# A four-layer encoder trunk: cross attention by products of high and low parts, one buffer for decay rows, six shared slots for weights

## What is computed

```python
def memory_cross_attention(q, mem_n, w_kv, gq, gk):
    k, v = jnp.split(mem_n @ w_kv, 2, axis=-1)
    q = rmsnorm(q.reshape(b, l, X_HEADS, X_HEAD_DIM), gq)
    k = rmsnorm(k.reshape(b, m, X_HEADS, X_HEAD_DIM), gk)
    v = v.reshape(b, m, X_HEADS, X_HEAD_DIM)
    s = jnp.einsum('blhd,bmhd->bhlm', q, k).astype(jnp.float32) * (X_HEAD_DIM ** -0.5)
    p = jax.nn.softmax(s, axis=-1).astype(v.dtype)
    return jnp.einsum('bhlm,bmhd->blhd', p, v).reshape(b, l, X_WIDTH)
```

## Time and profile before

| | us |
|---|---|
| median of three runs | 1771.86 |
| the profiled execution | 1771.1 |
| its span, first to last instruction | 1769.3 |
| TensorE busy | 1763.4 |
| VectorE busy | 1162.1 |
| ScalarE busy | 1004.8 |
| GpSimd busy | 220.8 |
| low parts of weights on VectorE, 569 of 1.226 us | 691.9 |
| casts of weights on ScalarE, 569 of 1.060 us | 597.0 |

### The profile page before, as it was taken

One profiled execution on the slowest core, in us unless ns is written; L12 is line 12 of the kernel. 1 busy time (PEld: TensorE's weight loads), 2 busy tenths in 40 slices (PEclk: granted clock), 3 DMA queues, 4 the chain that ended last, 5 costly groups with the idle time before them and its releaser, 6 DMA issues.

```text
span 1769.3 us, 25818 instructions
## 1 busy us (share of the span) xinstructions
PE 1763.4 (100%) x9492; PEld 1519.9 (86%) x9492; DVE 1162.1 (66%) x1596; ACT 1004.8 (57%) x1598; POOL 220.8 (12%) x548
## 2 busy tenths in 40 slices
PE   9999999999999999999999999999999999999999
PEld 8998988888888888888888888888899998888887
DVE  5788875655665665666666546666678887556665
ACT  6667775544455675544465545444566777545443
POOL 3412231000012230000012300000131223100000
PEclk9999999999999999999999999999999999999999
DMA  8565543566555443565655445666556554356663
GB/s 285 165 209 183 179 144 124 176 199 191 191 175 176 161 143 119 181 200 190 189 192 196 161 131 174 199 190 193 182 169 205 184 165 156 129 190 191 190 191 131
DMA packets 90041, 314.03 MB, mean 177 GB/s; under 512 B 10176, under 2 KB 11584, under 8 KB 89920
## 3 DMA queue, kind: packets, MB, share of 16 engines
q1 hardware_dynamic: 89328, 311.27, 54.4%
q10 hardware_dynamic: 592, 1.12, 0.2%
HBM read 311.23 MB, written 1.11 MB: 177 GB/s over the span
## 4 chain that ended last, share of the span: by engine, by line
PE 96%; DVE 2%; ACT 1%; issue 0%; DMA 0%; SPq 0%; DVEq 0%; ACTq 0%
PE ps L1229 19%; PE ps L1231 19%; PE ps L1230 19%; PE ps L1251 13%; PE ps L1258 7%; PE ps L1240 3%; PE ps L1241 3%; PE ps L1242 3%; PE ps L1396 2%; PE ps L1376 2%; PE ps L1327 1%; PE ps L1276 1%; PE ps L1286 1%; DVE w_lo_t L1669 1%; DVE xsT L1752 1%; DVE bcT L1752 1%
## 5 line engine op out<-in xcount | busy, mean ns | idle before, releaser
L1669 DVE TENSOR_TENSOR w_lo_t<-raw,w_hi_t 128x1024 fp32r<-128x1024 f32 x569 | 691.9, 1226 | 387.9 <-ACT w_hi_t L1425 387.4
L1425 ACT ACTIVATE w_hi_t<-raw 128x1024 fp32r<-128x1024 f32 x569 | 597.0, 1060 | 394.6 <-PE ps L1231 146.9
L1229 PE MATMUL ps<-w_hi_t,act_hi 128*128 128x512 f32 x832 | 329.2, 396 | 0.0
L1230 PE MATMUL ps<-w_lo_t,act_hi 128*128 128x512 f32 x832 | 324.2, 390 | 0.0
L1231 PE MATMUL ps<-w_hi_t,act_lo 128*128 128x512 f32 x832 | 324.1, 389 | 0.0
L1251 PE MATMUL ps<-hT,w_hi_t 128*128 128x512 f32 x1024 | 256.0, 392 | 0.0
L1251 PEld LDWEIGHTS ps<-hT,w_hi_t 128*128 128x128 f32 x1024 | 185.9, 189 | 34.4
L1231 PEld LDWEIGHTS ps<-w_hi_t,act_lo 128*128 128x128 f32 x832 | 156.2, 188 | 33.1
L1229 PEld LDWEIGHTS ps<-w_hi_t,act_hi 128*128 128x128 f32 x832 | 156.4, 188 | 31.2 <-issue 0.4
L1230 PEld LDWEIGHTS ps<-w_lo_t,act_hi 128*128 128x128 f32 x832 | 156.4, 188 | 30.6
L1229 PE MATMUL ps<-w_hi_t,hT 128*128 128x512 f32 x416 | 165.7, 398 | 0.0
(11 more groups left out here) (219 smaller groups left out, 2220.7 us busy)
## 6 DMA issues: line engine op xcount, KB each, us to landing
raw<-in_wstream SPq DMA_DIRECT2D x569, 512.0 KB, 3.8
gap<-cs_rows SPq DMA_DIRECT2D x32, 256.0 KB, 4.7
mix<-in_mem SPq DMA_DIRECT2D x4, 256.0 KB, 4.9
x<-in_x SPq DMA_DIRECT2D x1, 1024.0 KB, 9.3
raw<-in_wstream SPq DMA_DIRECT2D x2, 256.0 KB, 3.7
wsT<-in_sgu_wT ACTq DMA_DIRECT2D x1, 512.0 KB, 5.4
sgain<-in_sgu_gain ACTq DMA_DIRECT2D x1, 512.0 KB, 6.4
out<-x SPq DMA_DIRECT2D x1, 512.0 KB, 2.8
```

Source lines behind the costliest of these rows:

```text
L1229: pe.matmul(o, ah, wh[:, n], start=first and c == 0, stop=False)
L1230: pe.matmul(o, ah, wl[:, n], start=False, stop=False)
L1425: act.activation(w_hi_t[:, u % RING, :], raw[:, u % RING, :], ACT.Copy).then_inc(w_hi, 1)
L1669: dve.tensor_tensor(w_lo_t[:, u % RING, :], raw[:, u % RING, :], w_hi_t[:, u % RING, :].bitcast(F32), ALU.subtract)\
```

## The change

The scores and the values of the cross heads are each computed as three products of fp32r parts, high with high, high with low, low with high: 12 matmuls in place of 4. For this `qT`, `kT`, `v` and `xpT` become fp32r and get low parts, which DVE makes from the same PSUM bank once ACT has written the high part: `qT_lo` and `kT_lo` (in tiles of `act_hi` and `act_lo` that are free then), `v_lo` and `xpT_lo`. The jobs of these steps have two readers now. The low part of a weights unit is written over the raw unit, in one tensor of six slots; SP loads unit u when TensorE is through with unit u - 6. The decay rows have one buffer; SP loads a group's rows when the exponents of the group before are done, and the planner puts the subtraction three units behind the group's `ssd_a`. `COST` gets the new figures.

```diff
+SLOTS = 6
@@
-                tj = self.misc_job(True, False)
+                tj = self.misc_job(True, dst in ("qT", "kT"))
+                if tj.dve:
+                    self.work(0, 0.7, 0)
@@
-        job = self.stream_job(True, False)
+        job = self.stream_job(True, evac == "v")
@@
-        pT = self.misc_job(True, False)
+        pT = self.misc_job(True, True)
@@
             yield from rows(0)
-            self.spawn(rows(1))
@@
                 if g + 1 < SG:
-                    self.spawn(gaps(g + 1))
-                    self.spawn(weighted(g + 1), 1)
-                if g + 2 < SG:
-                    self.spawn(rows(g + 2), 1)
+                    self.spawn(rows(g + 1))
+                    self.spawn(gaps(g + 1), 3)
+                    self.spawn(weighted(g + 1), 3)
@@
-        raw = sb("raw", [P, RING, UNIT])
+        v_lo = sb("v_lo", [P, TT, D], F32R)
+        o_raw = here()
+        raw = sb("raw", [P, SLOTS, UNIT])
         w_hi_t = sb("w_hi_t", [P, RING, UNIT], F32R)
-        w_lo_t = sb("w_lo_t", [P, RING, UNIT], F32R)
+        w_lo_t = sb("w_lo_t", [P, SLOTS, UNIT], F32R, o_raw)
@@
-            for u in range(RING + 1, NU):
-                while row_steps and row_steps[0]["w"] <= u - RING - 1:
+            for u in range(SLOTS, NU):
+                while row_steps and row_steps[0]["w"] <= u - SLOTS + 1:
                     s = row_steps.pop(0)
                     n = s["n"]
                     sp.wait_ge(cs_out, 16 * (s["l"] + 1))
-                    if n > 1:
-                        sp.wait_ge(e_new, TT * (n - 1))
+                    if n:
+                        sp.wait_ge(e_new, TT * n)
...
-                sp.wait_ge(w_lo[plan.lo_on[u - RING]], plan.lo_n[u - RING])
+                kind, value = plan.release[u - SLOTS]
+                sp.wait_ge(w_used if kind == "used" else job_done, value)
                 weights(u)
@@
                         for c in range(2):
-                            mm = pe.matmul(ps[:, s["job"].banks[0], t * MEM:(t + 1) * MEM], qT[:, 2 * s["h"] + c, t * P:(t + 1) * P],
-                                           kT[:, 2 * s["h"] + c, :], start=c == 0, stop=c == 1, skip_group_check=True)
+                            d = 2 * s["h"] + c
+                            pe.matmul(o, qT[:, d, tok], kT[:, d, :], start=c == 0, stop=False, skip_group_check=True)
+                            pe.matmul(o, qT[:, d, tok], kT_lo[:, d, :], start=False, stop=False, skip_group_check=True)
+                            mm = pe.matmul(o, qT_lo[:, d, tok], kT[:, d, :], start=False, stop=c == 1, skip_group_check=True)
@@
-                    pe.wait_ge(act_free, s["pT"])
-                    pe.wait_ge(act_free, s["v"])
+                    split(s["pT"])
+                    split(s["v"])
...
@@
+                elif k == "x_turn":
+                    n = s["n"]
+                    dve.wait_ge(act_free, s["job"].act)
+                    dve.tensor_tensor(xpT_lo[:, n % 2, :], ps[:, s["job"].banks[0], :], xpT[:, n % 2, :].bitcast(F32), ALU.subtract).then_inc(dve_free, 1)
+                elif k == "evac" and s["evac"] == "v":
...
+                    dve.wait_ge(act_free, job.act)
+                    dve.wait_ge(r_new, s["r"][1])
+                    for t in range(TT):
+                        ins = dve.scalar_tensor_tensor(out=v_lo[:, t, c], in0=ps[:, job.banks[t], :], scalar=R[s["r"][0]][:, t:t + 1],
+                                                       in1=v[:, t, c].bitcast(F32), op0=ALU.mult, op1=ALU.subtract)
+                    ins.then_inc(dve_free, 1)
```

More of the change, by code:

```diff
@@ L248, in evac @@
         job.read_dve(self)
+        if evac == "v":
+            self.work(0, 1.4, 0)
         return self.step("evac", job=job, evac=evac, **kw)
@@ L314, in value @@
         if not self.units:
-            job = self.v_act[n] = self.stream_job(True, False)
+            job = self.v_act[n] = self.stream_job(True, True)
             def later():
@@ L353, in head @@
         job = self.misc_job(True, True)
-        self.step("x_out", n=n, h=h, pT=pT.act, v=self.v_act[h // 2].act, job=job)
+        self.step("x_out", n=n, h=h, pT=pT, v=self.v_act[h // 2], job=job)
         self.parts["cross", h] = job
@@ L719, in one @@
             jobs = [self.misc_job(False, True) for _ in range(2)]
-            self.step("d_score", h=h, qk=max(self.ready["dq", h // 4], self.ready["dk", h // 4]), jobs=jobs)
+            self.step("d_score", h=h, qk=max(self.ready["dq", h // 4].act, self.ready["dk", h // 4].act), jobs=jobs)
             yield 1, "d_exp"
@@ L934, in sem @@
             return ctx.enter_context(nc.semaphore(name))
-        raw_in = [sem(f"raw_in{s}") for s in range(RING)]
+        raw_in = [sem(f"raw_in{s}") for s in range(SLOTS)]
         w_hi, w_used = sem("w_hi"), sem("w_used")
@@ L941, in bass_trunk @@
         mem_in = [sem(f"mem_in{m}") for m in range(4)]
-        gap_in = [sem(f"gap_in{m}") for m in range(2)]
+        gap_in = sem("gap_in")
         zeros_in, w0_in, w_half, w0_lo = sem("zeros_in"), sem("w0_in"), sem("w_half"), sem("w0_lo")
@@ L1007, in weights @@
             def weights(u):
-                sp.dma_start(raw[:, u % RING, :], A["wstream"][u]).then_inc(raw_in[u % RING], 16)
+                sp.dma_start(raw[:, u % SLOTS, :], A["wstream"][u]).then_inc(raw_in[u % SLOTS], 16)
             g = mem_cols
@@ L1021, in _ @@
             sp.dma_start(x[:, :, :], x_rows).then_inc(x_in, 16)
-            sp.wait_ge(w_lo[plan.lo_on[0]], plan.lo_n[0])
-            weights(RING)
+            weights(4)
             sp.dma_start(pc[:, 0:g.start], A["percol"][:, 0:g.start]).then_inc(pc_in, 16)
@@ L1424, in cast_to @@
                     else:
-                        act.activation(w_hi_t[:, u % RING, :], raw[:, u % RING, :], ACT.Copy).then_inc(w_hi, 1)
+                        act.activation(w_hi_t[:, u % RING, :], raw[:, u % SLOTS, :], ACT.Copy).then_inc(w_hi, 1)
                     cast[0] += 1
@@ L1557, in _ @@
                         act.wait_ge(gap_new, TT * n + b + 1)
-                        act.activation(E[:, b, :], gap[n % 2][b][:, :], ACT.Exp).then_inc(e_new, 1)
+                        act.activation(E[:, b, :], gap[b][:, :], ACT.Exp).then_inc(e_new, 1)
                     act.wait_ge(dve_free, jobs["C"].dve)
@@ L1722, in _ @@
                             ins.then_inc(t0_lo, 1)
+                    ins.then_inc(dve_free, 1)
+                elif k == "nt_turn" and s["dst"] in ("qT", "kT"):
+                    job, tile = s["job"], s["tile"]
+                    b = job.banks[0]
+                    dve.wait_ge(act_free, job.act)
+                    if s["dst"] == "kT":
+                        ins = dve.tensor_tensor(kT_lo[:, tile:tile + 2, :].rearrange("p a b -> p (a b)"), ps[:, b, :],
+                                                kT[:, tile:tile + 2, :].rearrange("p a b -> p (a b)").bitcast(F32), ALU.subtract)
+                    else:
+                        i = s["gain"][1]
+                        for f in range(2):
+                            ins = dve.scalar_tensor_tensor(out=qT_lo[:, tile + f, :], in0=ps[:, b, f * SEQ:(f + 1) * SEQ],
+                                                           scalar=gx16[:, 2 * i + f:2 * i + f + 1], in1=qT[:, tile + f, :].bitcast(F32),
+                                                           op0=ALU.mult, op1=ALU.subtract)
                     ins.then_inc(dve_free, 1)
```

62 lines of the change are left out of this document (37 added, 25 removed).

## The result

The changed kernel takes 1807.35 us (median of four runs, 1804.92 to 1809.16), before took 1771.82 in the same session: 1.0201 times as long, 95% interval 1.0188 to 1.0214. It is slower by 35.5 us, where 4.5 us of gain were forecast. The profiled execution took 1809.16. One of the five executions of experiment 1's kernel took 2203.9 us at a mean clock of 0.75, where the other four took 1800.6 to 1801.9.

The account below looks back on a forecast made before the run. TensorE's list of matmuls was taken to bound the kernel. A saving of 9.2 us less waits of 2.5, 1.2 and 1.0 us gave -4.5 us, so 1767.4 us, range 1762.7 to 1772.0.

Parts of the forecast that it names:

- TensorE's saving: Scores and values of the cross heads: 0.29 us saved per head step, 9.2 us over 2 x 16 steps.
- the saving of 13.4 us: Rival for the cross heads' new products: isolated spacing of 0.109 us saves 13.4 us, giving 1763.2 us; chance 0.03.
- A: Second query block of the state-space layers: TensorE waits 0.75 us for a bank and 0.5 more, 1.25 us, twice.
- B: Last value block of layer 3, once: TensorE waits 1.2 us for a bank that VectorE reads after the values' low part.
- C: Head 1 of layer 0, once: the values wait 1.0 us for the bank of group 6's carried product.
- The step that failed: Check of the changed program's order for matmul groups whose bank is wanted too early; it found three kinds of place.
- Half a sentence on the decay rows: State-space groups: VectorE's subtraction stands three units behind the exponent's step, so row loads cost 0, ends 0 and 17 us.
- VectorE falls behind among the heads: Rival: half of twelve waits for low parts of attention weights or keys pay 0.8 us, adding 4.8: 1772.2 us; chance 0.17.
- The row loads hold the weights: Rival: weights queue behind SyncE's wait for the exponent, 1.2 us a group in 14 groups, 17 us: 1784 us; chance 0.07.
- about 1 us later than their gate asks: Weights queued behind the decay rows go out about 1 us late, with over 8 us in hand; cost taken as 0.
- Nine in a hundred for slower: Chance 0.09 of slower by over 3.5 us, above 1775.4 us: 0.07 + 0.01 and 0.01 of the lag's tail.
- The signs: SyncE's waits name TensorE, exponent wait near 40 us or more; TensorE busy near 1755 us, waits 4 to 6 us.

Follow-up runs that it names:

- experiment 1: Kernel before with only the one buffer for decay rows and the new place of the groups' steps: 1801.25 us, ratio 1.0166.
- Experiments 2 and 4: Changed kernel with the convolution's evacuation not held back for load: 1783.48 us; changed kernel with a group's gated output one unit earlier: 1786.67 us.
- experiment 7: Changed kernel with four planner delays altered: convolution's evacuation not held back; masked products, gated output and normed blocks' transposes one unit earlier: 1766.09 us, ratio 0.9969.
- experiment 5: Changed kernel with the planner's costs of before, the engines still doing all the new work: 1801.1 us, ratio 1.0166.
- second run: The kernel of experiment 1 run once more for its trace, against the kernel before: 1801.0 us.
- 6: Changed kernel with scores and values again as 4 f32 matmuls on the high parts, low parts still made and waited for: 1813.69 us.

## Why the prediction was wrong

**TensorE's saving was right.** 9.2 us forecast, 8.95 measured. The Trainium skill (TensorE: Matmul & The Clock Gate, section Back-to-back issue gap) gives N/2.4 + 2.5 ns for an isolated matmul; the saving of 13.4 us that was estimated from it is not there, and the spacing of 120 ns between the stream's matmuls gave the right size.

**Places A, B and C were right, in place and size.** In the changed kernel's timeline, the reader and the matmul that waited for it, at A, C and B:

```profile
258.65 1.65 DVE L1749 SCALAR_TENSOR_TENSOR act_hi<-ps,stats,qT 128x256 fp32r<-128x256 f32 x4
259.66 0.63 PE L1316 MATMUL ps<-consts_sb,xsT 128*128 128x128 f32 x4 [0.87 <-DVE act_hi L1749]
...
292.33 0.41 DVE L1842 TENSOR_TENSOR cbm<-ps,stats 128x256 f32<-128x256 f32 x1
292.80 0.39 PE L1410 MATMUL ps<-xpT,v 128*128 128x256 f32 x1 [0.64 <-DVE cbm L1842]
...
1545.66 1.41 DVE L1942 SCALAR_TENSOR_TENSOR v_lo<-ps,stats,v 128x512 fp32r<-128x512 f32 x2 [0.51 <-ACT v L1535]
1546.99 0.87 DVE L1836 TENSOR_TENSOR xs<-ps,xs 128x256 f32<-128x256 f32 x2
1547.46 0.39 PE L1410 MATMUL ps<-xpT,v 128*128 128x256 f32 x1 [0.97 <-DVE xs L1836]
```

At A the first wait ends with the second of VectorE's four steps (259.51 us), the scores wait for the fourth (260.30 us) and start at 260.40. From start to start A is 1.1 + 0.35 us (forecast 0.75 + 0.5) in both layers, C 0.9 (1.0), B 1.2 (1.2): 5.0 against 4.7. Two smaller ones (0.9 at 1564, 0.5 at 32 us) were not forecast.

**The step that failed** is the one behind the list of places: "for each matmul group, added up TensorE's own work between the last write of its bank and its next". It measures how much time the readers of a bank have, and leaves out when their turn comes. It found the banks that got a new reader or a shorter interval. In the longest stop the interval was as long as before, 14 us of TensorE's work (219.4 to 233.4 in the change, 212.4 to 226.5 before); what had moved was the reader, an old one that no line of the diff names. Half a sentence on the decay rows, that the subtraction stands three units on, was costed at nothing, since only the rows' transfer was looked at. Experiment 1 prices that half sentence, together with the one buffer, at 29 us.

**The mechanism in its place.** The groups' steps moved by up to three units, so VectorE's sum of work in the planner peaks elsewhere. This sum is the planner's own reckoning; VectorE itself had idle time ahead of the longest stop. The planner then holds what may be held, and the convolution's second half was one of these. Experiments 2 and 4 show it from both sides: with the hold lifted or with the sum changed, the 5.6 us are gone. That a held step was the last reader of two banks is nothing that the planner looks at. The groups also end later, so output parts of layer 0 are transposed directly ahead of their units (6.0 us with the one at 730).

**A second price was missing altogether:** the clock. Before it was 1.000 throughout, and every wait was costed as its own length. The stretches at the lower level add 9.9 us to the 34.6 of the waits.

**The rivals.** "VectorE falls behind among the heads" was forecast at 1772.2; TensorE's waits there are 0.7 us for a low part of attention weights. "The row loads hold the weights" had the right sign and the right part of the change, with the wrong mechanism: in the changed kernel no stop of TensorE behind 32 us goes back to a load. The forecast's "about 1 us later than their gate asks" was wrong all the same: in experiment 7 the first load behind the rows is some 5 us late and costs what is said there. Nine in a hundred for slower was too little because each case for it was one of transfers or of VectorE's total, none of the order.

**The signs.** SyncE's waits name TensorE and its wait for the exponent is 52.1 us, as forecast. TensorE's busy time is 1768.8 us where 1755 was said, and 1754.2 in experiment 7; most of the difference is the lower clock. The waits went over the 8 us that were named as a sign of error.

What stays open: which of the new cost entries moves the differential layer (they were taken out together), and how much of the 3.1 us there is the order and how much the work, since 0.8 at 645 and at 690 us remain in experiment 5.

## What to carry to other kernels

Where a program sets the order, cost a change by what it does to steps that it doesn't name: for each bank or buffer list the last reader's place in its engine's order and the next writer's, in both programs, and look at every distance that shrank. In these traces each wait of TensorE that is put down to "issue" ends 0.1 us after a read of VectorE from PSUM; so look for the instruction that ended just before. An evacuation can also be late because its engine stood waiting for weights: follow the chain back to the end before calling a late load harmless. And before giving up a change that lost, try the order: here four numbers turned 35.5 us of loss into 5.6 of gain.

## What the runs showed of the hardware

TensorE's clock fell behind stops that are short beside the kernel. Behind 5.4 us of idle time it was at 1.2 GHz for 3.5 us or more, in all eight such stops (two each in the changed kernel and in experiments 1, second run, 5 and 6), and that cost 1.7 to 3.0 us each. Behind stops with 1.8 to 2.0 us of idle time it fell in 8 of 19, and that cost 1.7 us each time; behind the 33 with 1.1 to 1.7 us it never did. The same stop can go either way: behind the one that ends at 190.6 us four spacings are as usual, 0.31 and three times 0.23 us, and the next eight are 0.40 to 0.43; at 1446 us, behind its twin in layer 3, the clock is 1.00:

```profile
190.00:195.00 5.00, 4.40 (x13) 3.37 (x14) 4.93 (x13) 0.83 (x1) 0.00 (x0) 0.66 0.26 99
...
1446.00:1450.00 4.00, 3.83 (x21) 3.31 (x22) 3.93 (x10) 0.76 (x2) 0.00 (x0) 1.00 0.27 110
```

The four runs of the changed kernel spread over 4.2 us, at mean clocks from 0.993 to 0.995, where those of before spread over 0.3 at 1.000; 0.002 of 1807 us is 3.6 us, so most of the spread goes with the clock.

A load of weights (512 KB) issued right behind a group's two loads of decay rows (256 KB each) took longer to land: 6.5 us in the median of the 16 in experiment 7, where the median of all weights' loads is 3.3.
